# Streaming the high and low part of x as one 512-column matmul

## The reference

```python
# first block, twice
proj = rms_norm(x, attn_norm[l]) @ w_in[l]                # 2048 x 3776: "input projection"
...                                                       # three attention mixers
x = x + mixed @ w_o[l]
h = rms_norm(x, mlp_norm[l])
x = x + jnp.square(jax.nn.relu(h @ w_up[l])) @ w_down[l]  # 2048 x 8192: "up"; 8192 x 2048: "down"
# second block, once, with 16 meta tokens ahead of the 256
proj = rms_norm(x, g) @ w_in_2        # queries, keys, values, state space input
...                                   # sliding attention, S5 state space, w_glu, w_out
x = x + jnp.square(jax.nn.relu(rms_norm(x, g) @ w_up)) @ w_down
```

## Time and profile before

| | us |
|---|---|
| median of 3 runs | 3368.91 |
| lowest and highest of them | 3367.3, 3370.2 |
| the profiled execution: its own time | 3362.63 |
| its span in the trace | 3360.8 |
| PE busy | 3255.0 (97%) |
| mean granted clock | 0.976 of 2.4 GHz |

### The profile page before, as it was taken

The page is one execution under the profiler, slowest core; times in us unless marked ns, Lnnn a source line. Parts: engine busy times, 40 slices in busy tenths (PEclk is TensorE's granted clock), DMA queues, the critical chain, the costliest instruction groups (busy, mean ns, idle before and its releaser), DMA issues.

```text
span 3360.8 us, 54404 instructions
## 1 busy us (share of the span) xinstructions
PE 3255.0 (97%) x20862; PEld 2938.8 (87%) x20862; DVE 1751.6 (52%) x2127; ACT 1401.1 (42%) x2059; POOL 856.0 (25%) x893
## 2 busy tenths in 40 slices
PE   7989999999999998999999999998899999999999
PEld 7977898989898897689898989988876998989897
DVE  4536645554545553665555454465455544444544
ACT  4334544434444433454343434441354433333343
POOL 1001634333422110154334252223010121203030
PEclk9989999999999999899999999998989999999999
DMA  6441455464555445045555555666422445455554
GB/s 224 175 175 56 178 198 206 176 220 182 206 192 217 180 181 198 16 184 187 210 194 206 186 216 182 219 224 210 147 76 101 175 178 198 179 196 182 193 188 162
DMA packets 66933, 602.58 MB, mean 179 GB/s; under 512 B 14720, under 2 KB 25088, under 8 KB 31696
## 3 DMA queue, kind: packets, MB, share of 16 engines
q1 hardware_dynamic: 53616, 590.40, 48.1%
q10 hardware_dynamic: 12752, 7.43, 0.8%
q0 software_dynamic: 400, 2.44, 0.2%
HBM read 582.09 MB, written 18.15 MB: 179 GB/s over the span
## 4 chain that ended last, share of the span: by engine, by line
PE 91%; DVE 3%; ACT 2%; issue 2%; DMA 1%; ACTq 1%; POOL 0%; DVEq 0%; SPq 0%; POOLq 0%
PE bank L638 90%; DMA raw<-stream 1%; PE bank L685 1%; ACT w_hi L1084 1%; DVE w_lo L1505 0%; ACTq L1340 0%; DVE proj L1711 0%; POOL cssb L2162 0%; DVE w_lo L1511 0%; ACT prob L1239 0%; DMA u<-urow 0%; DVE nmax L1677 0%; PE bank L733 0%; PE bank L968 0%; PE bank L843 0%
## 5 line engine op out<-in xcount | busy, mean ns | idle before, releaser
L638 PE MATMUL bank<-xg_hi,w_hi 128*128 128x256 f32 (+1 forms) x4352 | 1232.7, 283 | 9.0 <-DVE x L1542 4.3
L638 PE MATMUL bank<-xg_lo,w_hi 128*128 128x256 f32 (+1 forms) x4352 | 1234.0, 284 | 0.0
L638 PE MATMUL bank<-xg_hi,w_lo 128*128 128x256 f32 (+1 forms) x4352 | 1233.0, 283 | 0.0
L1084 ACT ACTIVATE w_hi<-raw 128x1024 fp32r<-128x1024 f32 x552 | 554.2, 1051 | 970.1 <-PE bank L638 970.1
L1505 DVE TENSOR_TENSOR w_lo<-raw,w_hi 128x1024 fp32r<-128x1024 f32 x480 | 624.3, 1342 | 537.6 <-ACT w_hi L1095 537.6
L638 PEld LDWEIGHTS bank<-xg_hi,w_hi 128*128 128x128 f32 x4352 | 831.6, 191 | 11.5 <-issue 5.1
L638 PEld LDWEIGHTS bank<-xg_hi,w_lo 128*128 128x128 f32 x4352 | 831.7, 191 | 0.0
L638 PEld LDWEIGHTS bank<-xg_lo,w_hi 128*128 128x128 f32 x4352 | 825.8, 190 | 0.9
L1095 ACT ACTIVATE w_hi<-raw 128x1024 fp32r<-128x1024 f32 x480 | 482.3, 1053 | 752.2 <-PE bank L638 752.2
L638 PE MATMUL bank<-w_hi,act_hi 128*128 128x512 f32 x1920 | 754.4, 393 | 1.9 <-DVE act_lo L1700 1.9
L638 PE MATMUL bank<-w_hi,act_lo 128*128 128x512 f32 x1920 | 750.2, 391 | 0.0
(11 more groups left out here) (306 smaller groups left out, 1953.3 us busy)
## 6 DMA issues: line engine op xcount, KB each, us to landing
raw<-stream SPq DMA_DIRECT2D x264, 2048.0 KB, 7.7
stabs<-ssm_tabs SPq DMA_DIRECT2D x8, 1176.0 KB, 9.5
rdo<-stabs SPq DMA_DIRECT2D x8, 768.0 KB, 6.7
ssm_bc<-smat SPq DMA_DIRECT2D x8, 640.0 KB, 11.5
stabs<-ssm_f SPq DMA_DIRECT2D x8, 512.0 KB, 10.8
drv<-stabs SPq DMA_DIRECT2D x8, 512.0 KB, 4.6
trig<-stabs SPq DMA_DIRECT2D x8, 408.0 KB, 8.9
x<-xrow ACTq DMA_DIRECT2D x4, 512.0 KB, 13.0
```

Of the source, the lines that this page charges most:

```text
L638: return pe.matmul(o, a, b, start=start, stop=stop, skip_group_check=True)
L1084: act.activation(hi[j][:, 8 * h:8 * h + 8, :], raw[r][:, 8 * h:8 * h + 8, P * j:P * j + P], ACT.Copy)\
```

## The change

`xg_hi` and `xg_lo` become the two halves of one tensor `xg`, and for the 260 tiles of 256 columns one matmul with w_hi streams both, 512 columns, into the whole bank: x_hi's sum in the left half, x_lo's in the right. The w_lo·x_hi matmul adds to the left half. The two halves are added when the bank is emptied: ACT copies the right half to SBUF (`low_to`), and DVE adds the left one to it (`fold`). The 12 tiles with meta tokens stay as they were.

The rest follows from that. In the up stages the hidden value stays in `hid[t]` (four buffers in place of two `relu` and two `rsq`): DVE folds, then between its two subtraction halves takes max(s, 0)·s in place, ACT rounds that to `act_hi`, POOL only subtracts. The norm is not in it: the square of 1/rms, per token (`rs2`), is a factor when the down projection is added to x. So `spread` is gone from the three up projections. In the input projection and for the queries `rstd` is multiplied in by a second DVE operation, between the halves.

```diff
-            def row_tile(b, j, rhs_hi, rhs_lo, k, first=0):
-                n = rhs_hi.shape[2]
-                mm(bank[b][:, 0:n], hi[j][:, k, :], rhs_hi[:, k, :], k == first, False)
-                mm(bank[b][:, 0:n], hi[j][:, k, :], rhs_lo[:, k, :], False, False)
-                return mm(bank[b][:, 0:n], lo[j][:, k, :], rhs_hi[:, k, :], False, k == (first - 1) % KT)
+            def paired_row(b, j, k):
+                o = bank[b][:, 0:2 * S].rearrange("p (e n) -> p e n", e=2)
+                mm(o, hi[j][:, k, :], xg[:, :, k, META:], k == 0, False)
+                return mm(bank[b][:, 0:S], lo[j][:, k, :], xg[:, 0, k, META:], False, k == KT - 1)
...
+            def low_to(T, b, dst):                        # ACT
+                act.wait_ge(tile_done, multiplied(T))
+                act.activation(dst, bank[b][:, S:2 * S], ACT.Copy).then_inc(low_out, 1)
...
             def up(...):                                  # ACT
                 T = T0 + 2 * T_UP * f + 4 * q + t
+                act.wait_ge(hlo_ready, H0 + T_UP * f + 4 * q + t + 1)
+                low_to(T, t, hid[t][:])
                 split(T + 2, ...)
                 act.wait_ge(evac_done, evacuated(T))
-                act.activation(act_hi[...], relu[t % 2][...], ACT.Square).then_inc(hhi_ready, 1)
+                act.activation(act_hi[...], hid[t][...], ACT.Copy).then_inc(hhi_ready, 1)
...
+                    project(2 * c + j, (2 * c + j) % 4)   # ACT, input projection: low_to ahead of each split
                     split(T0 + 2 * c + j + 2, c0 + (c + 1) // 2, (c + 1) % 2, j)
...
             for s in range(SLOTS):                        # ACT, second block
+                if s >= Q0:
+                    low_to(T_B2 + s, s % 2, q2[:, s - Q0, :])
                 split_after(T_B2 + s)
...
+            def fold(T, b, n, dst):                       # DVE
+                dve.wait_ge(tile_done, multiplied(T))
+                dve.wait_ge(low_out, n)
+                return dve.tensor_tensor(dst, bank[b][:, 0:S], dst, ALU.add).then_inc(folded, 1)
...
             def up(...):                                  # DVE
-                dve.wait_ge(tile_done, multiplied(T))
-                dve.wait_ge(hlo_ready, H0 + T_UP * f + 4 * q + t + 1)
-                dve.scalar_tensor_tensor(out=relu[t % 2][:], in0=bank[t][:, 0:S], scalar=0.0, in1=rstd[:, META:],
-                                         op0=ALU.max, op1=ALU.mult).then_inc(evac_done, 1)
+                fold(T, t, F, one)
                 for h in range(2):
+                    if h:
+                        dve.wait_ge(folded, F)
+                        dve.scalar_tensor_tensor(out=one, in0=one, scalar=0.0, in1=one, op0=ALU.max, op1=ALU.mult).then_inc(evac_done, 1)
                     split_half(T + 2, ..., h)
...
             def project(...):                             # DVE, input projection (queries: the same)
-                dve.tensor_tensor(proj[:, bass.ds(j, 1), :], one, rstd[...], ALU.mult).then_inc(evac_done, 1)
+                fold(T, b, F_LAYER * l + j + 1, one)
+                split_half(T + 2, r, e, 0)
+                dve.wait_ge(folded, F_LAYER * l + j + 1)
+                dve.tensor_tensor(one, one, rstd[:, META:], ALU.mult).then_inc(evac_done, 1)
+                split_half(T + 2, r, e, 1)
...
             def added(T, c, square=None):                 # DVE
-                    dve.tensor_tensor(one, bank[2 * (c % 2) + m][:], one, ALU.add).then_inc(evac_done, 2)
+                        dve.scalar_tensor_tensor(out=one, in0=bank[2 * (c % 2) + m][:], scalar=rs2[:, m:m + 1], in1=one,
+                                                 op0=ALU.mult, op1=ALU.add).then_inc(evac_done, 2)
...
             def ups(Tb, n=None):                          # PE
-                    if n is not None and t == 0:
-                        spread(n)
...
             def hidden(T0, H0, f):                        # POOL
-                        pool.tensor_tensor(rsq[t % 2][:], relu[t % 2][:], relu[t % 2][:], ALU.mult).then_inc(rr_ready, 1)
```

More of the change, by code:

```diff
@@ L144, in build @@
     xg_at = at[0]
-    xg_hi = place("xg_hi", [P, KT, L2], F32R)
-    xg_lo = place("xg_lo", [P, KT, L2], F32R)
+    xg = place("xg", [P, 2, KT, L2], F32R)
+    xg_hi, xg_lo = xg[:, 0], xg[:, 1]
     act_at = at[0]
@@ L167, in build @@
     ss, ssf = place("ss", [P, 2, NC]), place("ssf", [P, 2, NC])
-    stats = place("stats", [P, 6, 2])
-    st, sf, std, rs, xstd, xrs = [stats[:, i, :] for i in range(6)]
+    stats = place("stats", [P, 7, 2])
+    st, sf, std, rs, xstd, xrs, rs2 = [stats[:, i, :] for i in range(7)]
     qk_g = place("qk_g", [P, 1])
@@ L192, in build @@
     diag = place("diag", [P, 2, P], where=region)
-    relu = [place(f"relu{i}", [P, S], where=region) for i in range(2)]
-    rsq = [place(f"rsq{i}", [P, S], where=region) for i in range(2)]
+    hid = [place(f"hid{i}", [P, S], where=region) for i in range(4)]
     gfb_at = region[0]
@@ L654, in tile @@
                             before(k)
-                        last = row_tile(b, j, rhs_hi, rhs_lo, k)
+                        last = row(b, j, k)
                 last.then_inc(tile_done, 1)
@@ L719, in ups @@
                 for t in range(4):
-                    tile(Tb + t, t, t % 2, xh, xl, residual_ready(n, evacuated(Tb - 1)) if n is not None and t == 0 else None,
+                    tile(Tb + t, t, t % 2, residual_ready(n, evacuated(Tb - 1)) if n is not None and t == 0 else None,
                          bank_free(Tb + t, t))
-                    if n is not None and t == 0:
-                        spread(n)
                 with pe.Fori(1, C_UP // 2) as q:
                     for t in range(4):
-                        tile(Tb + 4 * q + t, t, t % 2, xh, xl)
+                        tile(Tb + 4 * q + t, t, t % 2)
             def ssm_tables(i):
@@ L1533, in rooted, with rooted_square, added, widened @@
                 last.then_inc(diag_ready, 1)
-                dve.wait_ge(spread_done, n + 1)
+                dve.wait_ge(spread_done, i + 1)
                 dve.tensor_copy(rstd[:, META:], bank[4][:, 0:S]).then_inc(rstd_ready, 1)
-            def added(T, c):
+            def rooted_square(i):
+                rooted(2 * i + 1)
+                dve.wait_ge(rs_ready, 3 * i + 2)
+                dve.tensor_tensor(rs2, rs, rs, ALU.mult).then_inc(rs_ready, 1)
+            def added(T, c, square=None):
                 dve.wait_ge(tile_done, multiplied(T))
+                if square is not None:
+                    dve.wait_ge(rs_ready, 3 * square)
                 for m in range(2):
                     one = x[:, m, W * c:W * c + W]
-                    dve.tensor_tensor(one, bank[2 * (c % 2) + m][:], one, ALU.add).then_inc(evac_done, 2)
-            def widened(Tb, each=None, then=split_half):
+                    if square is None:
+                        dve.tensor_tensor(one, bank[2 * (c % 2) + m][:], one, ALU.add).then_inc(evac_done, 2)
+                    else:
+                        dve.scalar_tensor_tensor(out=one, in0=bank[2 * (c % 2) + m][:], scalar=rs2[:, m:m + 1], in1=one,
+                                                 op0=ALU.mult, op1=ALU.add).then_inc(evac_done, 2)
+            def widened(Tb, each=None, then=split_half, square=None):
                 for c in range(NC):
@@ L1743, in _, with split_after @@
             rooted(4)
-            dve.wait_ge(rstd_ready, 5)
-            def split_after(T):
-                for h in range(2):
+            spread(2)
+            dve.wait_ge(rstd_ready, 3)
+            def split_after(T, halves=(0, 1)):
+                for h in halves:
                     if T + 2 < T_O2:
@@ L1752, in split_after, with out_of_psum, query_tile @@
                         split_wide_half(T + 2, (T + 2 - T_B2) // 2 % 2, T % 2, h)
-            def out_of_psum(T, b, dst, r):
+            def out_of_psum(T, b, dst):
                 dve.wait_ge(tile_done, multiplied(T))
-                dve.tensor_tensor(dst, bank[b][:, 0:dst.shape[1]], r, ALU.mult).then_inc(evac_done, 1)
+                dve.tensor_tensor(dst, bank[b][:, 0:L2], rstd[:], ALU.mult).then_inc(evac_done, 1)
+            def query_tile(i):
+                F = F_LAYER * DEPTH + i + 1
+                fold(T_B2 + Q0 + i, (Q0 + i) % 2, F, q2[:, i, :])
+                split_after(T_B2 + Q0 + i, (0,))
+                dve.wait_ge(folded, F)
+                dve.tensor_tensor(q2[:, i, :], q2[:, i, :], rstd[:, META:], ALU.mult).then_inc(evac_done, 1)
+                split_after(T_B2 + Q0 + i, (1,))
             def input_tile(i):
```

131 lines of the change are left out of this document (70 added, 61 removed).

## The result

The changed kernel takes 3340.68 us (median of 4 runs, 3336.99 to 3346.77) where the kernel before took 3369.55 beside it (3367.3 to 3372.33): 28.9 us less, a ratio of 0.9916 [0.9897, 0.9935]. The forecast was 3336.4.

The account below looks back on a forecast made before the run. PE, busy 97% of the span, was taken to bound the kernel. 40.2 - 2.0 - 1.4 + 0.35 - 1.6 - 3.0 = 32.5 us off 3368.91 gives 3336.4 us; range 3318 to 3370 for 8 in 10.

Parts of the forecast that it names:

- the term of 40.2 us: In the 260 tiles of 256 columns, one matmul for two saves 9.7 ns a group over 4160 groups, 40.2 us.
- I take the middle: Per group of matmuls, 9.7 ns saved, between bounds of 0 and another 9.7 ns (80 us in all).
- the causes that the prediction named for a smaller saving: At the paired matmuls: break in the operand costs more, 3412 us (chance 0.09); alternating lengths leave about 10 us, 3366 (0.05).
- emptying is hidden: Up tiles: the added ACT and DVE work costs nothing, with 2.8 us to spare; late-chain rival 3356 us, chance 0.04.
- tile 10: Input projection, two layers: savings of tiles 6 to 9 lost and the copy stands ahead of `csq`, -2.0 us.
- The forecast's two terms: Tile 10's wait: lost savings of four tiles, 4 x 0.155 us, and 0.4 us for the copy ahead of `csq`.
- the first up tiles: First up tiles of two layers: the pause moves from tile 1 to tile 2, -1.4 us for both layers.
- 0.7 a layer: First up tiles: tiles 0 and 1 win nothing and 0.4 us is added, -1.4 us for both layers.
- forecast 0.35: Second block's up projection, which has no tables: 0.35 us won without `spread`.
- the queries: Four places where PE waits for ACT behind its split: each gets the copy in front, -1.6 us in all.
- the clock falls: Pauses at tile 10 and up tile 2 grow: two falls to half clock at four places, -3.0 us.
- 8.0: Losses forecast at tile 10 (2.0), the first up tiles (1.4), the queries (1.6) and by the clock (3.0 us).

Follow-up runs that it names:

- order_alone: Kernel before with only its 256-column matmuls reordered, for two blocks together the w_hi ones, then the w_lo ones; 3333.48 us, ratio 0.9902.
- aligned_moved_64: aligned with 64 unused bytes ahead of x, so everything behind x moves too; 3486.89 us in one run beside one of 3376.5.
- same_length_grouped: two_and_two with each 512-column matmul made two of 256 again, so no length changes; 3330.15 us, ratio 0.9885.
- two_and_two: Changed kernel with the matmuls of two blocks together, in the order 512, 512, 256, 256; 3321.17 us, ratio 0.9855.
- contiguous_pair: Changed kernel with high and low x of a block side by side, so the 512-column operand is one piece; 3347.81 us, ratio 0.9937.
- four_and_four: two_and_two with its loops over 4 blocks: four matmuls of 512 columns, then four of 256; 3354.67 us, ratio 0.9957.
- emptying_alone: Changed kernel with each 512-column matmul undone into two of 256, all else as changed; 3370.88 us, ratio 1.0013 to the kernel before.
- changed_again: The changed kernel run once more, unaltered, for the spread from run to run; 3342.05 us, ratio 0.9915.
- changed_unrolled: Changed kernel with PE's loop over an up stage's last 12 tiles written out, same matmuls; 3347.34 us, ratio 0.9936.
- eight_and_eight: two_and_two with its loops over 8 blocks, the first tile of each projection at 4; 3349.3 us, ratio 0.994.
- aligned: Changed kernel with meta columns in their own tensor, x blocks 1024 instead of 1088 bytes apart, six matmuls a block in meta tiles; 3469.32 us, ratio 1.0299.

## Why the prediction was right, and where not

**Right: the size, nearly.** The forecast was 32.5 us less against a span; measured are 25.6 in the profiled execution and 28.9 in the medians. That it came so near is luck: the term of 40.2 us was 16 too large, and two other errors made up for most of it, 6.5 us of pauses that nobody had counted on and 5.4 us of losses that did not come.

**Wrong: 9.7 ns a group (the term of 40.2 us).** The measured 5.8 ns make 4160 x 5.8 = 24.1 us. The step that failed is "I take the middle, because each size keeps its own rate over hundreds of steps". 118.3 and 226.9 ns are not rates of a size: order_alone has 256-column matmuls at 115.1, aligned_moved_64 has 512-column ones of the down stage at 234. So 2 x 118.3 - 226.9 is no fixed part that a matmul costs. How little the pair saves in another order, two runs show: same_length_grouped and two_and_two, 88.31 and 88.22 us, 0.09 us over 256 pairs, 0.4 ns a pair. In the order of the kernel before it saved 5.8. How much of that is the fixed part and how much another order of the matmuls that are left can't be told, as the change alters both at once. The Trainium skill (TensorE: Matmul & The Clock Gate, Back-to-back issue gap), which has for a single matmul the columns and some 2.5 ns, would have given 10 us. The trace agrees in neither order: 5.8 ns a pair here, 0.4 in the other.

Neither of the causes that the prediction named for a smaller saving found support. Closing the break in the operand wins nothing (contiguous_pair is not shorter), and changes of length don't cost by themselves (same_length_grouped has none and gains, four_and_four has few and loses).

**Missed: the pauses at the third up stage, about 6.5 us.** The earlier trace rows had both in view, 2.09 and 2.57 us of idle with their releasers, and the prediction used them only for the clock. PE goes through the middle two pairs of an up and a down stage in one loop (`pe.Fori(1, FCH - 1)`), whose body holds 8 up tiles (4, and 4 in an inner loop), 16 down tiles and, in the first two layers, 24 small matmuls for the tables; the pause stood where this loop turns back, not at the short inner ones. Counted in the matmuls of one body, those of the inner loop once:

| | first two layers | second block |
|---|---|---|
| 256-column matmuls alone (before, emptying_alone, same_length_grouped, order_alone) | 384 + 24 + 384 = 792: pause | 384 + 384 = 768: none |
| 512 and 256 (changed, changed_again, contiguous_pair, two_and_two and the others) | 256 + 24 + 384 = 664: none | 640: none |
| changed_unrolled | 512 + 24 + 384 = 920: pause | 896: pause |

So every turn of a body of 792 or more has the pause and none of 768 or fewer has it, and unrolling brings it back with everything else left alone. That it hangs on the length of PE's code is shown. That PE waits for its instructions to be loaded is the likely reading, not shown: in the layers the records name a DVE write or subtraction as releaser, in the second block of changed_unrolled none. The down stages give back 2.25 and 2.73 us, the stretch at half clock behind the first pause another 1.5.

**Right: emptying is hidden.** Timelines of ACT and DVE around one up tile of the changed kernel, answering to the earlier trace rows; ACT first.

```profile
1003.01 0.38 ACT L1127 ACTIVATE hid<-bank 128x256 f32<-128x256 f32 x1 [2.16 <-PE bank L639]
1003.29 2.00 ACT L1087 ACTIVATE w_hi<-raw 128x1024 fp32r<-128x1024 f32 x2
...
1006.08 0.42 ACT L1138 ACTIVATE act_hi<-hid 128x256 f32 x1 [0.78 <-DVE hid L1614]
...
1003.43 0.42 DVE L1604 TENSOR_TENSOR hid<-bank,hid 128x256 f32<-128x256 f32 x1 [2.00 <-ACT hid L1127]
1004.38 1.23 DVE L1535 TENSOR_TENSOR w_lo<-raw,w_hi 128x1024 fp32r<-128x1024 f32 x1 [0.53 <-ACT w_hi L1087]
1005.52 0.42 DVE L1614 SCALAR_TENSOR_TENSOR hid<-hid 128x256 f32<-128x256 f32 x1
1005.86 1.22 DVE L1535 TENSOR_TENSOR w_lo<-raw,w_hi 128x1024 fp32r<-128x1024 f32 x1
```

The copy comes first, then the split; the first half is ready 2.6 us behind the copy's start (forecast 2.7 behind the tile's end), the second 4.1 (4.4). PE waits for nothing in the middle of an up stage.

**Right, and smaller: tile 10.** From the timelines of ACT, DVE and PE, from tile 5 to tile 10, answering to the earlier trace rows:

```profile
61.85 0.39 ACT L1127 ACTIVATE proj<-bank 128x256 f32<-128x256 f32 x1 [3.31 <-PE bank L639]
...
64.03 1.05 ACT L1223 ACTIVATE csq<-proj 128x1024 f32<-128x1024 f32 x1
...
81.17 3.35 DVE L1683 RECIPROCAL crstd<-cstd 128x512 f32<-128x512 f32 x1 [4.09 <-ACT cstd L1229]
...
85.99 0.50 PE L639 MATMUL bank<-xg,w_hi 128*128 128x512 f32 x1 [1.83 <-DVE w_lo L1535]
```

The wait grew from 1.04 to 1.83, by 0.79. The forecast's two terms, with 5.8 ns in place of 9.7, would give nearly that (4 x 0.09 for the tiles and 0.4 for the copy), but emptying_alone, whose tiles are as long as before, parts it otherwise:

```profile
86.70 0.39 PE L639 MATMUL bank<-xg,w_hi 128*128 128x256 f32 x1 [1.64 <-DVE w_lo L1535]
```

The new emptying makes 0.60 of it: `csq` starts 0.25 us later behind the end of tile 5, and POOL's sum behind it takes 1.27 us in place of 0.93. The faster tiles make only 0.19, half of what they save from tile 6 to 9; from POOL's second step to `cstd` the chain itself is 0.19 shorter (13.64 us, before 13.83), and why is open.

**Half right: the first up tiles.** The pause moved from tile 1 to tile 2, and the one for the diagonal is gone. Timelines of DVE and PE there, answering to the earlier trace rows; then the windows of PE behind this pause and behind tile 10 (stretch, busy, clock, DMA, GB/s):

```profile
408.13 1.23 DVE L1535 TENSOR_TENSOR w_lo<-raw,w_hi 128x1024 fp32r<-128x1024 f32 x1 [0.52 <-ACT w_hi L1087]
...
409.41 0.51 PE L639 MATMUL bank<-xg,w_hi 128*128 128x512 f32 x1 [1.60 <-DVE w_lo L1535]
...
86.00:89.40 3.40, 3.40 (x19) 1.00 0.00 0
409.40:412.80 3.40, 3.39 (x19) 1.00 0.00 0
```

But no 0.7 a layer were lost. What such a stage takes beyond a plain one was 3.12 us before and is 3.14 now, so it won as much as any other (96.56 to 95.09, from its start to the next stage's). The half that PE waits for took 1.23 us, not the 1.7 that the prediction had put in; this alone gives back 0.4 of it. In the second block, without tables, 0.37 were won (forecast 0.35).

**Right in place, too large: the queries.** PE's waits in the second block's projection of the changed kernel (us, times, longest), answering to the earlier trace rows:

```profile
PE bank L639 <- ACT ks L1406: 3.7, 1, 3.7
...
PE bank L940 <- ACT vm L1411: 2.9, 1, 2.9
...
PE bank L639 <- ACT ks L1415: 2.7, 1, 2.7
```

0.2 to 0.3 longer each, not 0.4.

**Wrong: the clock falls.** Two of four were taken (3.0 us); none came. The windows above show 1.00 behind the waits of 1.83 and 1.60 us. The waits stayed below 2.09, from which the guess was made, but that doesn't explain it: in contiguous_pair the clock fell behind both waits at tile 10, 1.80 us each, and tile 10 then took 1.5 us more. PE's timeline and window there, first layer:

```profile
84.82 0.50 PE L640 MATMUL bank<-xg,w_hi 128*128 128x512 f32 x1 [1.80 <-DVE w_lo L1535]
...
86.00:89.40 3.40, 3.40 (x13) 0.50 0.00 0
```

changed_unrolled and eight_and_eight lost it at one of the two (1.82 and 1.77 us), two_and_two at neither (1.96). In the nine profiled executions with waits of 1.77 to 1.96 us at tile 10 it fell at 4 of 18 places, and behind the waits at the first up tiles (1.45 to 1.71 us) at none. One in two was too high, but not by a size that is safe.

In sum: 24.1 for the groups instead of 40.2 and 6.5 for the pauses that were not seen; against that stand, instead of 8.0, about 2.6 (the input projections won 1.7 and, without the clock, 2.0 where 30 tiles at 5.8 ns a group make 2.8; the queries 0.7), and 0.4 were won in the second block. That makes 28.4, with the 1.3 of half clock in the second input projection 29.7. The trace's 25.6 lack some 4: the two attentions took 1.5 more than before, the second block up to its output projection 3.2 more, which is within what they vary by. Their cause is open.

## What to carry to other kernels

A step between matmuls that is the same for hundreds of steps is the rate of that stream of matmuls, its order above all, not a price of one matmul: before a saving is computed from the difference of two such rates, run one kernel that only reorders. Here the reordering alone, without any of the new layout, gave 33.5 us, and together with the paired matmul 48.4. Of what the pair adds to the reordering, 8.5 us are the two pauses of order_alone and the half clock behind them; an up stage gains 0.09. And where the engine that sets the time stands still at the turn of a long loop, count its instructions: making the body shorter can be worth something by itself (here 2.3 to 2.7 us a turn).

## What the runs showed of the hardware

- The step of float32r matmuls with a weight load each depends on their order. The same 768 matmuls of 256 columns take 90.74 us as hi·hi, hi·lo, lo·hi block by block and 88.31 with two blocks together.
- The steps repeat. By block within a tile, and again after 8 blocks, the steps behind 512 and 256 columns of the changed kernel are on average 229, 118, 230, 118, 232, 121, 233, 124, then 226, 118, 233, 117, 232, 113, 232, 117 ns; in contiguous_pair 234, 118, 229, 118 for each two blocks. In `aligned` single steps go round in threes (236 and 113, 233 and 117, 241 and 120) without regard to the block.
- The same stream at the same place has run at two rates in one execution: up stages of 89.20 and one of 90.33 us in aligned_moved_64, both at full clock and without idle time. What sets the rate is open.
- The place of the stationary operand can matter: 64 bytes changed the down stage from 86.94 to 89.46 us, 227 to 234 ns a matmul (one execution, all ten full stages). What makes the steps repeat and the place count stays open.
- At the turn of a loop whose body has 792, 896 or 920 matmuls PE started 2.3 to 3.0 us after its last matmul's start (1.9 to 2.6 us of idle time); with 640, 664 or 768 it went on after 0.23.
- The length of one stretch of idle time did not decide the clock. It fell to 0.50 after 1.77 (eight_and_eight), 1.80 (contiguous_pair, twice), 1.82 (changed_unrolled) and 2.09 us (before), and stayed at 1.00 after 1.60 and 1.83 (changed), 1.96 (two_and_two, twice) and 2.57 (before).
